# Mixer norm sums added on VectorE, output norm sums after the last product, and the first merge unit run under the last attention block

## What is computed

```python
x = x + 0.5 * swiglu(rmsnorm(x, norm_ffn1), ffn1_w_in, ffn1_w_out)
h = rmsnorm(x, norm_mix)
q_r, k_r, v_r, g_r, q_a, k_a, v_a, gate_r, gate_a = split(h @ w_in)
y_ret = retention_branch(q_r, k_r, v_r, g_r, ...)      # 4 heads, chunks of 128, both directions
y_att = window_attention_branch(q_a, k_a, v_a, ...)    # 8 query heads, 2 kv heads, blocks of 128
x = x + (sigmoid(gate_r) * y_ret + sigmoid(gate_a) * y_att) @ w_out
x = x + 0.5 * swiglu(rmsnorm(x, norm_ffn2), ffn2_w_in, ffn2_w_out)
return rmsnorm(x, norm_final)
```

## Time and profile before

| | us |
|---|---|
| median of three runs | 2041.87 (2038.05, 2041.87, 2041.9) |
| the profiled execution | 2038.59 |
| its span in the profile | 2036.8 |
| TensorE busy | 2000.8 |
| VectorE busy | 1318.5 |
| GpSimd busy | 888.3 |
| ScalarE busy | 739.4 |

### The profile page before, as it was taken

One profiled execution on the slowest core, in us unless ns is written; L12 is line 12 of the kernel. 1 busy time (PEld: TensorE's weight loads), 2 busy tenths in 40 slices (PEclk: granted clock), 3 DMA queues, 4 the chain that ended last, 5 costly groups with the idle time before them and its releaser, 6 DMA issues. The chain is left out here.

```text
span 2036.8 us, 25808 instructions
## 1 busy us (share of the span) xinstructions
PE 2000.8 (98%) x9160; PEld 1628.4 (80%) x9160; DVE 1318.5 (65%) x1477; ACT 739.4 (36%) x984; POOL 888.3 (44%) x564
## 2 busy tenths in 40 slices
PE   7999999999999999999999999999999999999998
PEld 5888888877888888888876668888788888877886
DVE  7866666678786434435686565457766666678775
ACT  6433333353344212221124554325333333353432
POOL 0343433578995222212221212242334434578992
PEclk9999999999999999999999999999999999999998
DMA  3332232465443111111211123331432332474532
GB/s 137 111 122 98 99 112 98 135 227 185 134 163 142 56 62 52 52 51 60 76 40 63 59 87 134 142 130 69 139 104 88 120 102 89 142 264 144 196 99 83
DMA packets 106865, 227.29 MB, mean 112 GB/s; under 512 B 9392, under 2 KB 30000, under 8 KB 106800
## 3 DMA queue, kind: packets, MB, share of 16 engines
q1 hardware_dynamic: 74816, 173.57, 24.7%
q10 hardware_dynamic: 31984, 52.86, 7.4%
HBM read 165.05 MB, written 61.34 MB: 111 GB/s over the span
## 5 line engine op out<-in xcount | busy, mean ns | idle before, releaser
L2085 POOL TENSOR_TENSOR w_lo<-stage,w_hi 128x1024 fp32r<-128x1024 f32 x54 | 136.6, 2531 | 436.9 <-ACT w_hi L1020 436.9
L1666 DVE SCALAR_TENSOR_TENSOR x<-ps,x 128x512 f32<-128x512 f32 x280 | 187.4, 686 | 101.9 <-PE ps L680 100.4
L611 PE MATMUL ps<-a_hi,w_hi 128*128 128x512 f32 x752 | 250.1, 400 | 1.2 <-DVE q_a L1853 0.6
L611 PE MATMUL ps<-a_hi,w_lo 128*128 128x512 f32 x752 | 242.7, 390 | 0.0
L611 PE MATMUL ps<-a_lo,w_hi 128*128 128x512 f32 x752 | 242.7, 390 | 0.0
L2100 POOL TENSOR_TENSOR gb<-gb,rstd 128x512 f32<-128x512 f32 x42 | 92.4, 2201 | 311.5 <-DVE gb L1597 292.3
L611 PEld LDWEIGHTS ps<-a_hi,w_hi 128*128 128x128 f32 x752 | 140.2, 188 | 37.5 <-issue 10.9
L611 PEld LDWEIGHTS ps<-a_hi,w_lo 128*128 128x128 f32 x752 | 141.4, 188 | 30.1
L611 PEld LDWEIGHTS ps<-a_lo,w_hi 128*128 128x128 f32 x752 | 141.7, 188 | 27.4
L680 PE MATMUL ps<-t_hi,hi 128*128 128x512 f32 x352 | 138.6, 394 | 7.3 <-DVE x L1666 6.9
L680 PE MATMUL ps<-t_hi,lo 128*128 128x512 f32 x352 | 137.1, 390 | 0.0
(11 more groups left out here) (321 smaller groups left out, 4569.3 us busy)
## 6 DMA issues: line engine op xcount, KB each, us to landing
stage<-wstream SPq DMA_DIRECT2D x56, 512.0 KB, 3.5
st_a<-win SPq DMA_DIRECT2D x42, 512.0 KB, 3.4
st_b<-win SPq DMA_DIRECT2D x42, 512.0 KB, 4.2
b_spill<-diff SPq DMA_DIRECT2D x82, 256.0 KB, 3.6
t_lo<-b_spill SPq DMA_DIRECT2D x40, 512.0 KB, 7.6
b_spill<-rawv SPq DMA_DIRECT2D x66, 256.0 KB, 4.1
a_lo<-b_spill SPq DMA_DIRECT2D x30, 512.0 KB, 5.1
x<-xT SPq DMA_DIRECT2D x16, 512.0 KB, 6.8
```

What stands on the lines that cost most here:

```text
L611: mm = pe.matmul(ps[:, bank, :], w[0:r, k, :], mv[0:r, k, HALF * half:HALF * half + HALF], start=first and part == 0, stop=final and part ...
L1666: dve.scalar_tensor_tensor(out=x[:, m, part], in0=ps[:, bank, :], scalar=0.5, in1=x[:, m, part], op0=ALU.mult, op1=ALU.add).then_inc(xacc, 1)
L2085: pool.tensor_tensor(w_lo[:, parity, :, :], stage[:, parity, :, :], f32(w_hi[:, parity, :, :]), ALU.subtract).then_inc(wlo_done, 1)
```

## The change

Three things. (1) VectorE adds all eight tiles of squares (ADDS = 7), as whole tiles (`add_tile`) for the mixer norm and as halves (`add_half`) for the last, so TensorE sums 8 chunks instead of 24 and `total` goes; `root` reads PSUM directly. (2) At the end both groups of sums stand after the last product, the order of ScalarE's last square and VectorE's reciprocal changes with them. (3) The first merge unit's k = 0 to 3 start right behind the last gate unit, with the last three transpositions behind k = 1 and the last values, now alternating between the kv halves, behind k = 2; for that `a_hi` and `a_lo` of `y_ret` are made tile by tile as the last gate unit releases them (`ret_high`, `ret_low`), those of `y_att` in a part of 896 tokens (`att_high`) and one of the last 128, straight from the values' bank. ScalarE's and VectorE's loops end before the last two blocks, which are written out. Cut to the core:

```diff
-ADDS = KT - 3
+ADDS = KT - 1
@@ tensor @@
-            def pass3(out_banks, k_range, parity, mhi, mlo, rows=None, ready=None, between=None):
+            def pass3(out_banks, k_range, parity, mhi, mlo, rows=None, ready=None, between=None, read=None):
...
+                    if read is not None and k < RH:
+                        last.then_inc(read, 1)
...
-            def sums_of_half(p, bank, h):
-                added_sums(p, bank, range(4 * h, 4 * h + 4))
-                for n in ((2, 3) if h == 0 else (0, 1)):
-                    mm = half_sums(p, bank, n)
-                mm.then_inc(sums_done, 1)
+            def sums_of_half(bank, h):
+                pe.wait_ge(acc_done, ACC_AT[3] + (ADDS if h == 1 else ADDS + 2))
+                column_sums(bank, 0, of_rstd, range(4 * h, 4 * h + 4)).then_inc(sums_done, 1)
...
-                    if f == 1 and s == NS - 1 and r == 6:
-                        sums_of_half(3, 6, 1)
...
-            for h in (1, 0):
-                sums_of_half(1, 4, h)
+            sums(1, 4)
...
-            def last_values(kv):
-                pe.wait_ge(pT_done, 6 * (CH - 1) + 3 * (kv + 1) + SEED)
+            def last_values():
+                pe.wait_ge(pT_done, 6 * CH + SEED)
                 for j in range(3):
-                    mm = value_part(0, kv, j)
-                return mm
+                    for kv in range(2):
+                        mm = value_part(0, kv, j)
+                mm.then_inc(pv_done, 1)
...
+            def last_block(k):
+                if k == 1:
+                    for j in range(3):
+                        turn_p(CH - 1, 1, j)
+                elif k == 2:
+                    last_values()
...
-            last_values(0)
-            for j in range(3):
-                turn_p(CH - 1, 1, j)
-            last_values(1).then_inc(pv_done, 1)
...
+            pe.wait_ge(exp_done, 2 * CH - 1 + (1 + SEED))
+            merge_unit(0, 0, lambda k: pe.wait_ge(alo_done, y_at + k + 1), last_block)
+            merge_unit(0, 1)
+            with pe.Fori(1, KT // 2) as i:
                 for b in range(2):
...
+                    merge_unit(i, b)
...
             ffn(1)
 
+            sums_of_half(6, 1)
             spread(4, 4, range(4, CH))
-            sums_of_half(3, 6, 0)
+            sums_of_half(6, 0)
             spread(5, 4, range(4))
@@ scalar @@
-                for n in range(2):
+                for n in range(2 if f == 0 else 3):
                     half_square(f, n)
                 if f == 1:
-                    act.wait_ge(total_done, 2)
-                    root(rinv[:, 4:CH], slice(4, CH))
+                    act.wait_ge(sums_done, 3)
+                    root(ps[:, 6, 4:CH], slice(4, CH))
...
-            act.wait_ge(total_done, 1)
-            root(rinv[:, :])
+            act.wait_ge(sums_done, 1)
+            root(ps[:, 4, 0:CH])
...
+            def ret_high(t):
+                act.wait_ge(gate_read, t + 1)
+                act.activation(a_hi[:, t, :], y_ret[:, t, :], ACT.Copy).then_inc(ahi_done, 1)
...
-                evac_pT(i, 0)
+                evac_pT(i, 0, after)
                 exps(i, 1)
...
-            with act.Fori(1, CH // 2) as it:
+            with act.Fori(1, CH // 2 - 1) as it:
...
+            attention_block(CH - 2, U_GATE + CH - 2, 0, CH - 3)
+            attention_block(CH - 1, U_GATE + CH - 1, 1, CH - 2, lambda j: ret_high(j) if j < 2 else None)
+            for t in range(2, RH):
+                ret_high(t)
...
+            def att_high(t):
+                act.activation(a_hi[:, RH + t, early], y_att[:, t, early], ACT.Copy).then_inc(att_hi, 1)
+
+            act.wait_ge(unit_done, U_MERGE)
+            act.wait_ge(yatt_done, CH - 1 + SEED)
+            for t in range(2):
+                att_high(t)
             evac_pT(CH - 1, 1)
             store_gate(CH - 1, U_MERGE - 1, 1)
...
+            for t in range(2, QA):
+                att_high(t)
+            act.wait_ge(pv_done, CH + SEED)
+            act.activation(a_hi[:, RH:2 * RH, late], ps[:, 0, :].rearrange("p (a n) -> p a n", a=QA), ACT.Copy
+                           ).then_inc(ahi_done, RH)
+            split(U_MERGE + 1, (U_MERGE + 1) % 2)
@@ vector @@
+            def add_half(f, n):
+                u, h = HALF_SQ[n]
+                part = (L, R)[h]
+                dve.wait_ge(sq_half, 4 * f + n + 1)
+                dve.wait_ge(acc_done, ACC_AT[2 * f + 1] + 5 + n)
+                dve.tensor_tensor(rstd[:, part], rstd[:, part], sq2[2 + u][:, h, :], ALU.add).then_inc(acc_done, 1)
+
+            def add_tile(f, u):
...
+                dve.tensor_tensor(two(rstd[:, :]), two(rstd[:, :]), sq2[2 + u], ALU.add).then_inc(acc_done, 1)
...
+                        if f == 1 and s == NS - 1 and n in (5, 2, 7):
+                            add_half(f, {5: 0, 2: 1, 7: 2}[n])
...
                 if f == 0:
                     for j in range(4, KT):
                         a_low(1, XK[j], KT + j)
+                    for u in range(2):
+                        add_tile(f, u)
+                else:
+                    recip(4, slice(4, CH))
+                    add_half(f, 3)
...
                 maxima(i, 1)
+                if last:
+                    for t in range(2):
+                        ret_low(t)
                 normalise(i, 1)
...
             dve.wait_ge(evac, U_MERGE)
...
+            for t in range(2, RH):
+                ret_low(t)
...
+            for t in range(QA):
+                dve.wait_ge(att_hi, t + 1)
+                dve.tensor_tensor(a_lo[:, RH + t, early], y_att[:, t, early], f32(a_hi[:, RH + t, early]), ALU.subtract)
+            dve.wait_ge(ahi_done, 2 * KT + 2 * RH)
+            dve.tensor_tensor(a_lo[:, RH:2 * RH, late], ps[:, 0, :].rearrange("p (a n) -> p a n", a=QA),
+                              f32(a_hi[:, RH:2 * RH, late]), ALU.subtract).then_inc(alo_done, RH)
...
                 scale_half(m, R, 5)
-                if m == 3:
-                    dve.wait_ge(sums_done, 5)
-                    total(6, 3, slice(0, 4))
-                elif m == 5:
+                if m == 2:
                     recip(5, slice(0, 4))
```

More of the change, by code:

```diff
@@ L959, in attention_block @@
                 pe.wait_ge(evac, n)
-                pass3((None, 1), range(KT), parity, a_hi, a_lo,
-                      between=lambda k: turn_p(i, 0, k) if k <= 2 else None).then_inc(unit_done, 1)
+                pass3((None, 1), range(KT), parity, a_hi, a_lo, between=lambda k: turn_p(i, 0, k) if k <= 2 else None,
+                      read=gate_read if i == CH - 1 else None).then_inc(unit_done, 1)
             pe.wait_ge(kmask_done, 4)
@@ L1255, in ffn_out @@
                         high(1, XK[j])
-                for n in range(2, 4):
+                for n in range(2 if f == 0 else 3, 4):
                     half_square(f, n)
@@ L1263, in ffn_out @@
                 else:
-                    act.wait_ge(total_done, 3)
-                    root(rinv[:, 0:4], slice(0, 4))
+                    act.wait_ge(sums_done, 4)
+                    root(ps[:, 6, 0:4], slice(0, 4))
             def ffn(f):
@@ L1295, in ffn @@
                     act.wait_ge(wlo_done, U_TAIL2 + 1)
-                    act.wait_ge(sums_done, 3)
+                    act.wait_ge(sums_done, 2)
                     root(ps[:, 5, 0:CH])
@@ L1421, in exps, with evac_pT @@
                 act.activation(esnk[:, :], snk[:, :], ACT.Exp).then_inc(exp_done, 1)
-            def evac_pT(i, kv):
+            def evac_pT(i, kv, after=None):
                 for j in range(3):
@@ L1426, in evac_pT @@
                     act.activation(pT[kv][:, j, :], ps[:, 6 + (3 * kv + j) % 2, :], ACT.Copy).then_inc(pT_done, 1)
+                    if after is not None:
+                        after(j)
+            def ret_high(t):
+                act.wait_ge(gate_read, t + 1)
+                act.activation(a_hi[:, t, :], y_ret[:, t, :], ACT.Copy).then_inc(ahi_done, 1)
             def store_gate(i, n, b):
@@ L1437, in output, with attention_block @@
                                ACT.Copy).then_inc(yatt_done, 1)
-            def attention_block(i, n, b, before):
+            def attention_block(i, n, b, before, after=None):
                 split(n + 1, (U_GATE + b + 1) % 2)
@@ L2000, in normalise, with ret_low, attention_block @@
                                   rden[:, :].unsqueeze(2).to_broadcast([P, GRP, 3 * P]), ALU.mult).then_inc(p_done, 1)
-            def attention_block(i, n, b, stored_gates):
+            def ret_low(t):
+                dve.wait_ge(ahi_done, 2 * KT + t + 1)
+                dve.tensor_tensor(a_lo[:, t, :], y_ret[:, t, :], f32(a_hi[:, t, :]), ALU.subtract).then_inc(alo_done, 1)
+            def attention_block(i, n, b, stored_gates, last=False):
                 raw = (gs, sg)[b]
@@ L2016, in _ @@
                 attention_block(b, U_GATE + b, b, 16 * (RH + SEED))
-            with dve.Fori(1, CH // 2) as it:
+            with dve.Fori(1, CH // 2 - 1) as it:
```

(11 more changed lines are left out.)

54 lines of the change are left out of this document (16 added, 38 removed).

## The result

| | before | after |
|---|---|---|
| median of five runs, us | 2040.87 (2037.29 to 2041.9) | 2029.12 (2028.1 to 2032.36) |
| span of the profiled execution, us | 2036.8 | 2026.3 |

The ratio after to before is 0.9948, 95% interval 0.9938 to 0.9959: faster by 0.5%. The spans differ by 10.5 us, where 10.6 was forecast. The median is 0.5 us under the 2029.6 that was given.

What follows compares the result with a forecast made beforehand. TensorE, busy 2000.8 of 2036.8 us, was taken as the bound; 4.7 + 4.0 + 1.9 = 10.6 us gave 2028.0 from the profiled execution, 2031.3 from the median; forecast 2029.6, the middle, range 2025.6 to 2035.4.

Steps and rivals of the forecast that it cites:

- Place A: Norm before the mixer: 48 column sums become 16, the clock stays full, dense work resumes earlier; gain 4.7 us.
- "VectorE first" half of the rival: Norm before the mixer: VectorE takes the port before GpSimd, or adds fit beside it; sum 12.5, time 2027.7, chance 0.14.
- The clock rival: Norm before the mixer: clock still falls, so the gain there is 1.4; sum 7.3, time 2032.9, chance 0.24.
- drain: Rival: after the table load the norm's root comes 1.4 us later; sum 9.2, time 2031.0, chance 0.03.
- Place B: Between the last gate unit and the merge's k=4: values overlap and k-steps fill waits; gain 4.0 us.
- Of this 2.8 is the overlap of the values: Before the merge: alternating the two 64-column halves of the value matmuls gives 2.8 of the 4.0 us gain.
- The first wait: Start of the first merge unit: TensorE waits about 0.35 us for ScalarE's last exponentials (exp_done).
- The stall before the third transposition: In the first merge unit: TensorE waits 0.6 us for ScalarE's copy of the first transposition, queued behind four other copies.
- the merge unit's waits would eat B: Rival: ScalarE's in-order waits stop TensorE, merge gain 1 us or less; sum 7.6, time 2032.6, chance 0.07.
- Place C: Kernel's end: sums behind the last product, scalings start 1.0 us earlier and the 0.88 idle goes; gain 1.9.
- Peeled code: Rival: ScalarE pauses 14.62 us on first meeting peeled code in attention's last block; +4.0, time 2044.2, chance 0.03.
- behind it nothing is nearer: After the mixer norm's spread: seven k-steps (9.5 us) still cover VectorE's rope and q rotation, so no new wait.

Runs made afterwards that it cites:

- both kernels with 48 records: The kernel before (2040.87 us), and that kernel with only the attention and merge part changed (2037.09 us beside 2039.5, ratio 0.9984).
- the second test: Changed kernel with kv 0's value matmuls ahead of the last three transpositions and kv 1's behind the third k-step: 2032.11 us, one execution.
- the two edits: Changed kernel with the mixer norm's spread one k-step later and the third retention unit's weight split ahead of the spread's copy: together 2027.5 us, ratio 0.9941.

## Why the prediction was right

The mechanism of each part came true but for what is named below. That the sum was met within 0.05 us is luck in part: the parts missed by +0.35, -0.45 and +0.15, which cancel, and C's share depends on when the clock falls in the kernel before.

**Place A: right, 4.7 forecast, 5.05 measured.** Counted from the first column sum, the table load was placed 3.22 us later and came at 2.94, and the spread came 1.86 behind it, not 2.05 (root, reciprocal and hand-overs are shorter); it then took 1.80 and not 1.65. That VectorE's adds would queue up behind GpSimd was wrong in the order but not in the sum: three instructions of 1.2, 1.2 and 2.4 us that don't run together end at the same time in any order. So the "VectorE first" half of the rival came true and its price did not; that rival was priced as if order saved time. The Trainium skill (SBUF — State Buffer, "Who interferes with whom") says that the order of issue decides which of the two engines blocks the other. The blocking agrees with the 3236 ns, and the order doesn't: GpSimd's, which began at 658.19, was passed by an add that started at 659.27.

**The clock rival did not come true.** No trace of the kernels in which VectorE makes the mixer norm's adds shows a fall at A; both kernels with 48 records have it (669.7 and 667.9, each 4.8 us behind the start of the sums). What was right is that a shorter sparse stretch, broken by a dense k-step, keeps the 2.4 GHz. How near it is to losing it was not tried.

**The table load has no drain behind it.** It starts at 667.50 for 1.28 us and the root at 668.80, 0.02 later; nor is there a gap ahead of it, since the last exponential (666.86 for 0.63) ended at 667.49. By the drain of about 1.38 us that the Trainium skill (ScalarE: Activation LUTs, "What ACT_TABLE_LOAD costs") adds, the root would have started at 670.16. The trace does not agree, here as in the earlier trace rows.

**Place B: right in kind, a little over, 4.0 forecast, 3.55 measured.** The term "Of this 2.8 is the overlap of the values" measured 2.86 in the second test. The first wait measured 0.37 (0.35 forecast); the profile names no releaser for it, but the exponentials' last instruction, esnk, ended at 1197.46, 0.21 us before TensorE went on, so the forecast cause fits. The stall before the third transposition was 0.25 (0.6 forecast). The shorter stall gave nothing, since the first two transpositions took 1.04 us (1200.51 to 1201.55, where the stall begins) and not 0.7: from their start to k=2 it is 1.70, as forecast. The term that was mis-sized is the single k-steps, priced at 1.36 and (with its hand-over) 1.5 us: k=2, between transpositions and values, took 1.57 (1202.21 to 1203.78), and k=3 behind the values 1.63 (1206.50 to 1208.13). That is 0.34 of the missing 0.45; the start of the unit and k=0 and 1 add 0.08 each, the values came 0.08 and the transpositions 0.04 shorter, and 0.06 is the rounding of 3.94 to 4.0. A k-step that stands alone between other kinds of matmuls was priced too low. The prediction's list of the kernel before had a like error: its 12 transposition records, priced at 1.05 us, take 1.45 in the kernel after (1200.51 to 1202.21 less the stall), so less of the 14.4 us was waiting than it says; the waits that the trace before shows there are 0.25, 0.69 and 0.56. That the merge unit's waits would eat B did not come true, but all that the early unit earns beyond the values is 0.69 us, where 1.2 was forecast.

**Place C: right, 1.9 forecast, 2.05 measured.** The first scaling is 1.0 earlier against the dense work (4.87 us behind the last product's start, 5.87 before), as forecast, and the 0.88 us pause is gone. The second spread ran at half clock, which the working had allowed for.

**Peeled code** shows no pause: ScalarE's first peeled copy of `y_ret` starts within the transpositions of the last block, and TensorE waits nowhere for over 0.37 us at B. The 14.62 us of the earlier trace rows stands in the kernel after as well; its cause was not looked into.

**The parts add.** 10.65 us over three places against 10.5 between the spans. The prediction's "behind it nothing is nearer" held for the change, but with nothing to spare: taking the 1.44 us wait away only moved it to the third unit (stretch A not shorter), until sinr was freed too.

## What to carry to other kernels

Alternate matmuls of the two 64-column halves, and look for places where another kind of work separates them: here that alone was worth 2.86 us, four times what filling the waits with an early unit earned. When a wait is removed and the time stands still, look for the next wait on the same chain and take both away in one run: the two edits gave nothing and 0.24 us alone and 1.65 together. Judge edits under 2 us by the distance between two landmarks of the trace, since the executions differ by more than that for reasons elsewhere.

## What the runs showed of the hardware

- Six value matmuls (twelve records) took 2.79 us when the halves alternate, 3.71 in two runs back to back, and 2.79 + 2.79 with transpositions between. The records of the two halves run in pairs, all of them in the first case, four of six in the second, none in the third.
- The order in which VectorE and GpSimd get the ports they share was not the order in which they began: in all twelve traces with the two adds GpSimd's subtraction, begun first behind a running VectorE instruction, let another VectorE instruction pass (1.22 us) and took 4.56 us in all, where it takes 2.4 alone.
- In some executions TensorE runs at 1.2 GHz for a few us near 485 and 1840 us, in code that is the same in all these kernels, and in others not (0.57 against 1.00 over 484 to 488). Each of these falls follows a wait of about 2 us for VectorE; the same wait without a fall is in other traces.
